# Prompt attention of a hybrid decoder step: which operand of the probability–value product is stationary, and who scales and gates its result

## The chip, the cores and the metric

The kernel runs on one core of a Trainium2 chip. The metric is the device time of one execution in microseconds; the median of three runs is quoted. The core has a matrix engine (TensorE, "PE" in the profile, its weight loads "PEld"), VectorE ("DVE"), ScalarE ("ACT"), GpSimd ("POOL") and a queue engine that issues transfers ("SP"). A matmul takes one operand as stationary weights, loaded by a LDWEIGHTS, and streams the other, the moving one, through them.

## The reference, cut to what matters

For every prompt token an indexer chooses 256 earlier tokens; attention then runs over the chosen ones only. Each query head (8 heads, 2 key/value heads, 128 wide) is normalised by its softmax, and the result is gated by `silu(z_b)`:

```python
logits = einsum('btkgd,btnkd->btkgn', qg, k_sel) * HEAD_DIM ** -0.5
logits = where(valid, logits, NEG_INF)
p = softmax(logits, axis=-1)
o = einsum('btkgn,btnkd->btkgd', p, v_sel)
...
branch_b = attend(q, qi, wi, k, v, ki) * silu(z_b)
merged = sigmoid(g_a) * (branch_a @ w_pa) + sigmoid(g_b) * (branch_b @ w_pb)
```

The sequence has 2048 tokens and the model is 1024 wide. Beside the prompt, 8 sequences of 8 new tokens with a paged cache go through the same layer.

## The kernel before

The prompt is worked through in four tiles of 512 tokens (t = 0 to 3). For each tile TensorE runs 97 products of the big projections, the indexer, and the attention stage that the change touches. Instead of gathering the chosen keys, the kernel computes dense causal logits and adds a mask.

The attention stage of a tile has 16 units u: four query blocks of 128 tokens times four pairs of heads. A unit of query block b of tile t sees n = 4t + b + 1 key blocks of 128, so over the four tiles there are 544 pairs of a unit and a key block. For each unit:

- TensorE forms the logits of both heads (`head_logits`), in pieces of up to 512 keys in three rotating PSUM banks; VectorE adds the mask, writes them to `LP` and takes the row maximum (`mask_logits`, L1835, L1840); ScalarE exponentiates (L900) and sums each row (`SUM`).
- TensorE turns the probabilities, 128x128 at a time, by matmuls with the identity (`turn_p`, L1053, tile `LP`), two key blocks (four turns) to a chunk; ScalarE (L924) or VectorE (L1872) copies each chunk from PSUM to one of three buffers `T`.
- TensorE multiplies (`head_values`): the values `V` of a key block are stationary and the turned probabilities of both heads, 256 columns, are moving (tile `T,V`). The result is already transposed, head dimension by tokens, in columns 0 to 255 of PSUM bank 6 or 7. All of this is plain fp32, for which the trace shows two loads and two matmuls for each call; the big projections are split by hand into high and low halves and show one load and one matmul for each.
- Division by the row sum: VectorE takes the reciprocal `RIN` and builds two diagonal matrices `DG` (L1863); TensorE multiplies them with a matrix of ones (tile `DG,ones`), which spreads 1/sum over all partitions into columns 256 to 511 of the bank; ScalarE copies that to `RB` (L908); VectorE multiplies result and `RB` into `BB` (`finish`, L1846); GpSimd multiplies `BB` by the gate `SZB` (`attn_gate`, L2115).

Each engine has its own program, with semaphores between them; the order on each engine is the order of the text. On TensorE it is `head_logits(u+1)`, inside which the first chunk of unit u is turned, and then `head_values(u)`. On VectorE it is `mask_logits(u+1)`, reciprocal, `DG`, VectorE's share of the copies of unit u, `finish(u-1)`, and, in the first eight units of the last tile, a part of the mask selection of a later block (`choose`, L1754 to L1760).

After the last unit `attn_high` (ScalarE, L942) and `attn_low` (GpSimd L2126, VectorE L1885) split `BB` into `BBH` and `BBL`, eight slices k of which two belong to each head pair, and TensorE goes on with the products `pb` (tile `BBH,WLH`), slice after slice. GpSimd takes slices 0 and 2, then the gate of the last unit, then 4 and 6. The loading of the next tile's input waits for `attn_z`, the mark of the gate of the last unit.

Of the kernel before, what the change touches and what calls it, by code (L numbers as in the profile page):

```python
# [33 lines left out]
ALU = mybir.AluOpType  # L34
# [3 lines left out]
P = 128  # L38
# [72 lines left out]
def program(nc, ins, outs, plan):  # L111
# [78 lines left out]
    DG = [at(f"DG{i}", [P, 256], F32, rJ + 2048 + 1024 * i) for i in range(2)]  # L190
# [111 lines left out]
    for u in range(NSEQ // 2 + 1):  # L302
        for c in range(4):
# [40 lines left out]
    qk, logits, row_max, expd, diag, p_t, p_copy, p_copy_a, pv, rb, rb_copy, attn, attn_z = (  # L344
        signal(n) for n in ("qk", "logits", "row_max", "expd", "diag", "p_t", "p_copy", "p_copy_a", "pv", "rb",
                            "rb_copy", "attn", "attn_z"))
# [270 lines left out]
    def _(act):  # L617
# [275 lines left out]
        def attend(t):  # L893
            for u in range(len(UNITS) + 1):
# [8 lines left out]
                if u >= 1:  # L903
                    v = u - 1
                    act.wait_ge(*rb.at(t, v))
                    if v >= 2:
                        act.wait_ge(*attn.at(t, v - 2))
                    act.activation(RB[v % 2][:, :], ps[6 + v % 2][:, 256:512], ACT.Copy).then_inc(*rb_copy.mark(t, v))  # L908
# [122 lines left out]
    def _(pe):  # L1031
# [364 lines left out]
        def head_values(t, u):  # L1396
# [9 lines left out]
            for c in range(groups):  # L1406
# [3 lines left out]
                if c == 0:  # L1410
                    claim(acc)
                for kk in range(min(2, n - 2 * c)):
                    k = 2 * c + kk
                    ins_ = mm(ps[acc][:, 0:256], V[:, k, (pr // 2) * HD:(pr // 2 + 1) * HD],
                              T[p_slot(t, u, c)][:, kk * 256:(kk + 1) * 256], k == 0, k == n - 1)
                ins_.then_inc(*pv.mark(t, u, c))
            pv.values[t, u] = pv.n
            pe.wait_ge(*diag.at(t, u))
            mm(ps[acc][:, 256:512], ones[:, :], DG[u % 2][:, :]).then_inc(*rb.mark(t, u))
            freed[acc] = attn.at(t, u)  # L1420
# [20 lines left out]
        for t in range(TILES):  # L1441
# [18 lines left out]
            for u in range(len(UNITS)):  # L1460
                if u + 1 < len(UNITS):
                    head_logits(t, u + 1)
                head_values(t, u)
            for f in range(KC):
# [21 lines left out]
    def _(dve):  # L1486
# [355 lines left out]

        def finish(t, u):
            blk, pr = UNITS[u]
            dve.wait_ge(*rb_copy.at(t, u))
            dve.tensor_tensor(BB[:, 2 * pr:2 * pr + 2, blk * P:(blk + 1) * P],  # L1846
                              ps[6 + u % 2][:, 0:256].rearrange("p (h q) -> p h q", h=2),
                              RB[u % 2][:, :].rearrange("p (h q) -> p h q", h=2), ALU.mult).then_inc(*attn.mark(t, u))

        def attend(t):  # L1850
            dve.wait_ge(*gate_mul.at(t, KC - 1, "P"))

            dve.wait_ge(*product.at(len(GEMMS) // TILES * t + len(PROJ_A) + len(PROJ_B) - 1, last_part(t)))
            mask_logits(t, 0)
            for u in range(len(UNITS)):
# [4 lines left out]
                if u >= 2:  # L1860
# [376 lines left out]
```

## Time and profile before

| | |
|---|---|
| median of three runs | 3474.61 us (3470.73 to 3475.79) |
| profiled execution, its own time | 3464.39 us |
| its span, first to last instruction | 3462.5 us |
| mean granted TensorE clock | 0.983 of full speed |
| busy: PE / PEld / DVE / ACT / POOL | 96% / 78% / 61% / 34% / 26% |

Busy times of PE come from modelled ends, which overlap: what one matmul takes from the engine is read from the distance between two starts. In a timeline, a line with "xN" stands for N instructions, and its length reaches from the first start to the last end.

### The profile page before, as it was taken

How to read it: one execution, taken by the hardware profiler on the slowest of the kernel's cores; microseconds unless marked ns; L12 is line 12 of the kernel's file. 1: busy time of each engine (PE TensorE's matmuls, PEld its weight loads, DVE VectorE, ACT ScalarE, POOL GpSimd, SP SyncE). 2: the span in 40 equal slices, each digit the busy share in tenths (PEclk: the TensorE clock that was granted, in tenths of full speed). 3: DMA queues.
4: the chain of work that ended last, by engine and by line, in shares of the span. 5: the costliest groups of instructions: out<-in, count | busy, mean ns of one | idle time of the engine just before them, and what ended most of it. 6: DMA issues, size and time to landing. Idle time of an engine off the chain costs nothing.

```text
span 3462.5 us, 44323 instructions
## 1 busy us (share of the span) xinstructions
PE 3323.2 (96%) x16733; PEld 2704.4 (78%) x16733; DVE 2105.5 (61%) x3980; ACT 1167.2 (34%) x2141; POOL 886.0 (26%) x833
## 2 busy tenths in 40 slices
PE   7899999997889999999999999999999999999999
PEld 6778888864678788888777688888877588878887
DVE  3463399412553799404526999725525999997652
ACT  2345433333532422116412521144322722115531
POOL 2225574443550033101310132011210033110111
PEclk9999999999999999999999999999999999999999
DMA  8556576776377455661465255630375055660007
GB/s 231 181 194 200 171 244 228 258 252 225 110 239 234 138 182 192 211 225 39 168 202 195 87 194 200 231 126 12 111 232 196 33 192 192 215 224 10 10 20 239
DMA packets 281013, 592.29 MB, mean 171 GB/s; under 512 B 17725, under 2 KB 199159, under 8 KB 231138
## 3 DMA queue, kind: packets, MB, share of 16 engines
q1 hardware_dynamic: 270434, 551.70, 47.3%
q0 software_dynamic: 10368, 37.75, 3.2%
q8 instruction: 135, 2.21, 0.3%
q14 instruction: 76, 0.62, 0.1%
HBM read 448.93 MB, written 140.47 MB: 170 GB/s over the span
## 4 chain that ended last, share of the span: by engine, by line
PE 77%; DVE 13%; ACT 3%; DMA 3%; issue 2%; POOL 1%; SPq 1%; ACTq 0%; DVEq 0%; POOLq 0%
PE ps L1048 71%; DVE JUNK L1730 7%; PE ps L1053 6%; DVE SC L1672 1%; DMA WR<-in_w_in 1%; ACT T L717 1%; DVE SMALL L1734 0%; ACT sKPT L846 0%; POOL BBL L2126 0%; DMA GB<-gb_scratch 0%; DVE GE L1732 0%; DVE PFX L1756 0%; DMA WR<-in_w_proj_b 0%; SPq L440 0%; ACT JUNK L636 0%
## 5 line engine op out<-in xcount | busy, mean ns | idle before, releaser
L1048 PE MATMUL ps<-HTH,WLH 128*128 128x512 f32 x4672 | 1478.0, 393 | 0.0
L1048 PEld LDWEIGHTS ps<-HTH,WLH 128*128 128x128 f32 x4672 | 878.6, 188 | 187.2 <-issue 6.5
L1048 PE MATMUL ps<-HTL,WLH 128*128 128x512 f32 x2336 | 910.4, 390 | 0.0
L1730 DVE TENSOR_SCALAR_CACHE_REDUCE JUNK<-SC,SMALL 128x384 bf16<-128x384 f32 (+13 forms) x392 | 579.9, 1479 | 15.7 <-POOL sSC L2047 1.8
L1048 PEld LDWEIGHTS ps<-HTL,WLH 128*128 128x128 f32 x2336 | 439.5, 188 | 94.1 <-issue 6.5
L1835 DVE CUSTOM_DVE_ANT_0 LP<-ps,SC 128x512 f32<-128x512 f32 (+3 forms) x320 | 187.5, 609 | 344.9 <-PE ps L1048 281.8
L787 ACT ACTIVATE T<-ps 128x512 f32<-128x512 f32 x192 | 115.2, 600 | 691.7 <-PE ps L1048 691.7
L1985 POOL TENSOR_TENSOR WLH<-WR,WLH 128x1024 fp32r<-128x1024 f32 x97 | 233.4, 2406 | 404.2 <-ACT WLH L626 403.9
L1048 PE MATMUL ps<-T,V 128*128 128x256 f32 x1088 | 282.8, 387 | 5.6 <-ACT T L924 5.5
L1048 PEld LDWEIGHTS ps<-T,V 128*128 128x128 f32 x1088 | 187.3, 191 | 34.4 <-ACT T L924 12.6
L626 ACT ACTIVATE WLH<-WR 128x1024 fp32r<-128x1024 f32 x97 | 102.7, 1059 | 287.7 <-DMA WR<-in_w_in 209.6
L1605 DVE RECIPROCAL RS<-RS 128x512 f32<-128x512 f32 x40 | 134.1, 3351 | 89.4 <-ACT RS L701 89.2
L924 ACT ACTIVATE T<-ps 128x512 f32<-128x512 f32 (+1 forms) x200 | 115.7, 580 | 198.8 <-PE ps L1053 197.8
L1053 PE MATMUL ps<-ident,LP 128*128 128x128 f32 x1088 | 167.1, 275 | 4.4 <-ACT LP L900 4.4
L1048 PE MATMUL ps<-BBH,WLH 128*128 128x512 f32 x512 | 162.4, 393 | 7.0 <-POOL BBL L2126 6.9
L1048 PE MATMUL ps<-MGH,WLH 128*128 128x512 f32 x512 | 166.7, 398 | 0.0
L717 ACT ACTIVATE T<-ps 128x512 f32<-128x512 f32 (+3 forms) x304 | 153.9, 549 | 33.1 <-DVE QI L1651 8.3
L1048 PE MATMUL ps<-BAH,WLH 128*128 128x512 f32 x512 | 164.0, 392 | 0.0
L1672 DVE SCALAR_TENSOR_TENSOR SC<-T,WI,SC 128x512 f32<-128x512 f32 (+3 forms) x266 | 161.2, 676 | 2.8 <-ACT T L717 1.4
L1053 PEld LDWEIGHTS ps<-ident,LP 128*128 128x128 f32 x1088 | 135.0, 141 | 33.3 <-DVE SMALL L1835 4.7
L2039 POOL TENSOR_SCALAR_AFFINE_SELECT SC<-SC 128x128 f32<-128x128 f32 x16 | 4.6, 292 | 605.7 <-DVE SMALL L1718 605.4
L900 ACT ACTIVATE LP<-LP,SMALL 128x128 f32<-128x128 f32 (+15 forms) x128 | 152.3, 1194 | 4.9 <-DVE SMALL L1840 4.7
(316 smaller groups left out, 5045.8 us busy)
## 6 DMA issues: line engine op xcount, KB each, us to landing
WLH<-w_scratch SPq DMA_DIRECT2D x291, 1024.0 KB, 4.8
w_scratch<-WLH SPq DMA_DIRECT2D x97, 1024.0 KB, 6.3
WR<-in_w_in SPq DMA_DIRECT2D x73, 512.0 KB, 4.4
MW<-in_w_mod SPq DMA_DIRECT2D x24, 512.0 KB, 7.2
XN<-in_x_prompt SPq DMA_DIRECT2D x4, 2048.0 KB, 7.9
q_scratch<-QO SPq DMA_DIRECT2D x32, 256.0 KB, 5.6
ma_scratch<-T SPq DMA_DIRECT2D x32, 256.0 KB, 5.6
gb_scratch<-GB SPq DMA_DIRECT2D x32, 256.0 KB, 6.4
```

The costliest lines, as they stand in the source:

```text
L626: act.activation(WH[j % 3][:, :, :], WR[j % 3][:, :, :], ACT.Copy).then_inc(*w_high.mark(j))
L717: act.activation(T[1 + r % 4][:, 0:n], ps[bank("idx", t, b, h, c)][:, 0:n], ACT.Relu).then_inc(*relu.mark(r))
L787: act.activation(dst, src, func).then_inc(*evac.mark(j, p))
L900: ins_ = act.activation(row, row, ACT.Exp, bias=NM[:, u % 2, hh:hh + 1], accum_out=SUM[:, u % 2, hh:hh + 1])
L924: act.activation(T[p_slot(t, u, c)][:, 0:m], ps[bank("tr", t, u, c)][:, 0:m], ACT.Copy).then_inc(*p_copy_a.mark(t, u, c))
L1048: return pe.matmul(out, lhsT, rhs, start=start, stop=stop, **more)
L1053: return pe.transpose(out, in_, ident[a:a + n, a:a + n])
L1605: link(dve.reciprocal(rs, rs))
L1672: dve.scalar_tensor_tensor(dst, x, w, dst, ALU.mult, ALU.add).then_inc(*scored.mark(r))
L1730: link(dve.tensor_scalar(JUNK[0:n, 0:row.shape[1]], row, MID[0:n, c:c + 1], 0.0, ALU.is_ge, ALU.add, accum_out=CNT[0:n, c:c + 1]))
L1835: ins_ = dve.tensor_tensor_reduce(LP[:, u % 2, hh, c:c + n], ps[bank("qk", t, u, hh, c)][:, 0:n], scores(t)[:, blk, c:c + n], 1.0, -3e38, ...
L1985: pool.tensor_tensor(WL[j % 3][:, :, :], WR[j % 3][:, :, :], WH[j % 3][:, :, :].bitcast(F32), ALU.subtract).then_inc(*w_split.mark(j))
```

## The change

The operands of the probability–value product change places: the turned probabilities of one head (128x128) are stationary, and the values of a key block (128 columns) are moving. The result now stands tokens by head dimension, so that 1/sum is a scalar of each partition. VectorE scales it so while copying it to a buffer `OB` (`scale`), TensorE turns it back (`turn_out`, two turns for each unit), and VectorE gates it with `SZB` while moving it to `BB` (`finish`). The diagonals, the matmuls with ones, ScalarE's copies to `RB` and GpSimd's gate are gone. At the start of the stage VectorE waits for `evac` in place of `product` of the last projection, since `finish` now reads `SZB`.

```diff
-    DG = [at(f"DG{i}", [P, 256], F32, rJ + 2048 + 1024 * i) for i in range(2)]
+    OB = [at(f"OB{i}", [P, 256], F32, rJ + 2048 + 1024 * i) for i in range(2)]
...
-                if u >= 1:
-                    v = u - 1
-                    act.wait_ge(*rb.at(t, v))
-                    if v >= 2:
-                        act.wait_ge(*attn.at(t, v - 2))
-                    act.activation(RB[v % 2][:, :], ps[6 + v % 2][:, 256:512], ACT.Copy).then_inc(*rb_copy.mark(t, v))
...
                 for kk in range(min(2, n - 2 * c)):
                     k = 2 * c + kk
-                    ins_ = mm(ps[acc][:, 0:256], V[:, k, (pr // 2) * HD:(pr // 2 + 1) * HD],
-                              T[p_slot(t, u, c)][:, kk * 256:(kk + 1) * 256], k == 0, k == n - 1)
+                    for hh in range(2):
+                        ins_ = mm(ps[acc][:, hh * HD:(hh + 1) * HD], T[p_slot(t, u, c)][:, (2 * kk + hh) * P:(2 * kk + hh + 1) * P],
+                                  V[:, k, (pr // 2) * HD:(pr // 2 + 1) * HD], k == 0 and hh == 0, k == n - 1, skip_group_check=True)
                 ins_.then_inc(*pv.mark(t, u, c))
             pv.values[t, u] = pv.n
-            pe.wait_ge(*diag.at(t, u))
-            mm(ps[acc][:, 256:512], ones[:, :], DG[u % 2][:, :]).then_inc(*rb.mark(t, u))
-            freed[acc] = attn.at(t, u)
+
+        def turn_out(t, u):
+
+            acc = 6 + u % 2
+            pe.wait_ge(*scaled.at(t, u))
+            for hh in range(2):
+                ins_ = turn(ps[acc][:, 256 + hh * P:256 + (hh + 1) * P], OB[u % 2][:, hh * HD:(hh + 1) * HD])
+            ins_.then_inc(*turned.mark(t, u))
+            freed[acc] = attn_z.at(t, UNITS[u])
...
                     head_logits(t, u + 1)
+                if u:
+                    turn_out(t, u - 1)
                 head_values(t, u)
+            turn_out(t, len(UNITS) - 1)
...
+        def scale(t, u):
+            dve.wait_ge(*pv.at(t, u))
+            for hh in range(2):
+                ins_ = dve.tensor_scalar(OB[u % 2][:, hh * HD:(hh + 1) * HD], ps[6 + u % 2][:, hh * HD:(hh + 1) * HD],
+                                         RIN[:, u % 2, hh:hh + 1], None, ALU.mult)
+            ins_.then_inc(*scaled.mark(t, u))
+
         def finish(t, u):
             blk, pr = UNITS[u]
-            dve.wait_ge(*rb_copy.at(t, u))
+            dve.wait_ge(*turned.at(t, u))
             dve.tensor_tensor(BB[:, 2 * pr:2 * pr + 2, blk * P:(blk + 1) * P],
-                              ps[6 + u % 2][:, 0:256].rearrange("p (h q) -> p h q", h=2),
-                              RB[u % 2][:, :].rearrange("p (h q) -> p h q", h=2), ALU.mult).then_inc(*attn.mark(t, u))
+                              ps[6 + u % 2][:, 256:512].rearrange("p (h q) -> p h q", h=2),
+                              SZB[:, 2 * pr:2 * pr + 2, blk * P:(blk + 1) * P], ALU.mult).then_inc(*attn_z.mark(t, UNITS[u]))
...
-            dve.wait_ge(*product.at(len(GEMMS) // TILES * t + len(PROJ_A) + len(PROJ_B) - 1, last_part(t)))
+            dve.wait_ge(*evac.at(len(GEMMS) // TILES * t + len(PROJ_A) + len(PROJ_B) - 1, last_part(t)))
...
                 link(dve.reciprocal(RIN[:, u % 2, :], SUM[:, u % 2, :]))
-                if u >= 2:
-                    dve.wait_ge(*rb.at(t, u - 2))
-                for hh in range(2):
-                    ins_ = dve.tensor_scalar(DG[u % 2][:, hh * P:(hh + 1) * P], ident[:, :], RIN[:, u % 2, hh:hh + 1], None, ALU.mult)
-                ins_.then_inc(*diag.mark(t, u))
+                if u:
+                    finish(t, u - 1)
...
-                if u:
-                    finish(t, u - 1)
                 for b, r in late_runs(t, u):
                     choose(t, scores(t)[:, b, 0:width(BLOCKS * t + b)], P, b, b, r)
+                scale(t, u)
...
-        def attn_gate(t, u):
-            blk, pr = UNITS[u]
-            pool.wait_ge(*attn.at(t, u))
-            x = BB[:, 2 * pr:2 * pr + 2, blk * P:(blk + 1) * P]
-            pool.tensor_tensor(x, x, SZB[:, 2 * pr:2 * pr + 2, blk * P:(blk + 1) * P], ALU.mult).then_inc(*attn_z.mark(t, UNITS[u]))
...
             attn_low(t, 2)
-            attn_gate(t, len(UNITS) - 1)
             attn_low(t, 4)
```

## Rows read from the trace of the kernel before

**Rows 1.** The profile page: the span, and busy time of PE.

```profile
span 3462.5 us, 44323 instructions
PE 3323.2 (96%) x16733; PEld 2704.4 (78%) x16733; DVE 2105.5 (61%) x3980; ACT 1167.2 (34%) x2141; POOL 886.0 (26%) x833
```

**Rows 2.** Windows, the attention stages of tiles 0 and 3: length, busy times, clock.

```profile
core 0: us, PE busy (x) PEld busy (x) DVE busy (x) ACT busy (x) POOL busy (x), PEclk, DMA share, GB/s
866.00:937.00 71.00, 58.55 (x288) 46.91 (x288) 40.56 (x162) 46.57 (x129) 33.81 (x44) 0.90 0.25 81
...
3110.00:3366.00 256.00, 246.97 (x1345) 210.12 (x1346) 167.38 (x455) 126.31 (x186) 24.56 (x31) 0.98 0.05 15
```

**Rows 3.** Timeline, inside a unit of tile 3: start, length, engine, operation.

```profile
3343.15 0.60 PE L1053 MATMUL ps<-ident,LP 128*128 128x128 f32 x4
...
3343.59 1.03 PE L1048 MATMUL ps<-T,V 128*128 128x256 f32 x4
...
3344.45 0.60 PE L1053 MATMUL ps<-ident,LP 128*128 128x128 f32 x4
```

**Rows 4.** Timeline, the end of a unit of tile 3: matmuls with ones, next turns.

```profile
3352.01 0.59 PE L1048 MATMUL ps<-DG,ones 128*128 128x256 f32 x2
...
3352.45 1.04 PE L1053 MATMUL ps<-ident,LP 128*128 128x128 f32 x8
```

**Rows 5.** Groups by form over the whole span: count, busy us, mean ns.

```profile
L1048 PE MATMUL ps<-T,V 128*128 128x256 f32 x1088 | 282.8, 387 | 5.6 <-ACT T L924 5.5
...
L1048 PE MATMUL ps<-DG,ones 128*128 128x256 f32 x128 | 39.9, 394 | 3.7 <-DVE DG L1863 3.4
...
L2115 POOL TENSOR_TENSOR BB<-BB,SZB 128x256 f32<-128x256 f32 x64 | 49.5, 774 | 336.3 <-DVE BB L1846 336.1
...
L1863 DVE TENSOR_SCALAR DG<-ident,SMALL 128x128 f32<-128x128 f32 x128 | 38.0, 338 | 2.3
...
L908 ACT ACTIVATE RB<-ps 128x256 f32<-128x256 f32 x64 | 24.3, 380 | 66.0 <-PE ps L1048 65.9
```

**Rows 6.** Timeline, three places: loads and matmuls with few moving columns.

```profile
42.41 7.16 PE L1048 MATMUL ps<-MW,SCT 128*9 128x128 f32 x64
...
878.12 0.27 PE L1048 MATMUL ps<-KLOW,QHIGH 128*128 128x128 f32 x1
...
878.23 0.28 PE L1048 MATMUL ps<-KHIGH,QLOW 128*128 128x128 f32 x1
...
880.86 0.28 PE L1048 MATMUL ps<-KLOW,QHIGH 128*128 128x256 f32 x1
...
880.98 0.29 PE L1048 MATMUL ps<-KHIGH,QLOW 128*128 128x256 f32 x1
...
881.99 0.30 PEld L1048 LDWEIGHTS ps<-T,V 128*128 128x128 f32 x2 [0.36 <-ACT T L924]
```

**Rows 7.** Waits of TensorE, attention stage of tile 0: us in total, times, longest.

```profile
PE ps L1048 <- DVE DG L1863: 3.4, 5, 1.1
```

**Rows 8.** Timeline, two places in tile 3: VectorE behind the end of a unit.

```profile
3335.62 0.59 PE L1048 MATMUL ps<-KHIGH,QHIGH 128*128 128x512 f32 x1
...
3336.82 0.69 DVE L1835 CUSTOM_DVE_ANT_0 LP<-ps,SC 128x512 f32<-128x512 f32 x1 [2.13 <-PE ps L1048]
...
3168.25 0.69 DVE L1835 CUSTOM_DVE_ANT_0 LP<-ps,SC 128x512 f32<-128x512 f32 x1 [3.57 <-PE ps L1048]
```

**Rows 9.** One line's instructions: VectorE's scaling in the sample attention, ns min/median/max.

```profile
L1793 DVE TENSOR_SCALAR RB<-ps,SMALL x4: 349/350/351, 798.3 to 862.6; 128x128 f32<-128x128 f32 x4
```

**Rows 10.** Timeline, from the last unit of tile 3 to the product `pb`.

```profile
3363.81 3.52 POOL L2126 TENSOR_TENSOR BBL<-BB,BBH 128x512 fp32r<-128x512 f32 x2
...
3365.73 0.47 PE L1048 MATMUL ps<-BBH,WLH 128*128 128x512 f32 x1 [1.57 <-POOL BBL L2126]
...
3367.29 1.18 POOL L2115 TENSOR_TENSOR BB<-BB,SZB 128x256 f32<-128x256 f32 x1
...
3369.76 0.50 PE L1048 MATMUL ps<-BBH,WLH 128*128 128x512 f32 x1 [0.72 <-POOL BBL L2126]
```

More of the change, by code:

```diff
@@ L343, in program @@
         signal(n) for n in ("u_ready", "taps", "conv", "ba_high", "ba_ready", "gate_mul"))
-    qk, logits, row_max, expd, diag, p_t, p_copy, p_copy_a, pv, rb, rb_copy, attn, attn_z = (
-        signal(n) for n in ("qk", "logits", "row_max", "expd", "diag", "p_t", "p_copy", "p_copy_a", "pv", "rb",
-                            "rb_copy", "attn", "attn_z"))
+    qk, logits, row_max, expd, p_t, p_copy, p_copy_a, pv, scaled, turned, attn_z = (
+        signal(n) for n in ("qk", "logits", "row_max", "expd", "p_t", "p_copy", "p_copy_a", "pv", "scaled", "turned", "attn_z"))
     k_high, k_split, k_whole = (signal(n) for n in ("k_high", "k_split", "k_whole"))
@@ L2186, in _ @@
                     split_low(AFTER_PAGES[u - 4])
-                if u:
-                    attn_gate(t, u - 1)
                 if u == len(UNITS) - 2 and t + 1 < TILES:
```

## The prediction, as it was put on record

> **What bounds the kernel now.** I read the page first: TensorE is busy for 3323.2 of 3462.5 us [rows 1], and the reader is to see that hardly any other engine's time can matter unless TensorE waits for it. Then the windows of the four attention stages: 71, 126, 186 and 256 us, 639 us together, of which the first and the last are shown [rows 2]. TensorE is busy for 247 of 256 us in the last, but only for 58.6 of 71 us in the first, so tile 0 is the one with waits. Since busy times overlap, I then took distances between starts in a timeline. In a full chunk of tile 3, four turns take 3343.59 - 3343.15 = 0.44 us, 0.11 each, and the four probability–value matmuls 3344.45 - 3343.59 = 0.86 us, 0.215 each [rows 3]; together 1.30 us without a gap. So the stage is priced by counting TensorE's instructions, and beyond that only the waits in tile 0 and the hand-over after the last unit are worth reading.
>
> **The probability–value product.** Before: 1088 matmuls of 256 columns [rows 5] at 0.215 us, 233.9 us. After: each becomes two, since a stationary block holds one head: 2176 matmuls of 128 columns, each with its own load, where there were 1088 loads. The columns streamed are the same, but loads double, so the price hangs on whether a load still hides. The trace of before does not show this form (fp32, a full 128x128 load, 128 moving columns). Its parts are there. With a load of only 9 columns, 64 fp32 matmuls of 128 columns take 7.16 us, first start to last end, and one lasts 0.27: (7.16 - 0.27) / 63 = 0.109 us each, the streaming alone. Two full fp32 loads, `T,V`, take 0.30 us, of which one lasts 0.19: the second starts 0.11 us after the first, the loading alone. Split-half matmuls with a full load and 128 columns start 878.23 - 878.12 = 0.11 us apart; with 256 columns 880.98 - 880.86 = 0.12 us [rows 6]. The latter is the pattern in which streaming and loading are equally long, as they would be here, and it shows some friction. Bounds: 0.109 (237.2 us, +3.3) and 0.12 (261.1 us, +27.2). I take 0.111, close to the three rows at 0.11, because the fp32 `T,V` rows at 0.215 for two passes over 256 columns show no friction with the loads beside them: 241.5 us, +7.6.
>
> On whether loads hide at all, the 0.11 us of the split-half matmuls with 128 columns answers: loading 0.11 and streaming 0.06 (half of the 256-column distance) one after the other would be 0.17. A sentence of the Trainium skill speaks against this change: its page "TensorE: Matmul & The Clock Gate", section "The mechanism" of Part 3, says that a weight load overlaps running matmuls only where it targets another row group, and every load here fills all rows. By that rule the sum would be that of the third rival; the trace does not agree, by the 0.11 us.
>
> **The matmuls with ones go.** 64 pairs, 128 matmuls [rows 5], 3352.45 - 3352.01 = 0.44 us each [rows 4]: 28.2 us. In the last unit of each tile TensorE stands waiting for GpSimd right behind the pair [rows 10], so there its removal gives nothing: 28.2 - 1.8 = -26.4 us.
>
> **The turns back come.** 64 pairs at 0.22 us, by the turns of the chunk [rows 3]: 14.1 us; those of the four last units lie in the same wait (0.9): +13.2 us. They need `scaled(u-1)`. Behind them on TensorE stand the turns and values of unit u, for which the copies on ScalarE and VectorE wait. VectorE scales as soon as the values of u-1 end, while TensorE runs all logits of unit u+1, so the wait should cost nothing. Bounds: nothing saved or lost below, and one exposed scaling above (next paragraph).
>
> **VectorE.** Two diagonals of 0.34 us mean [rows 5] go, two scalings from PSUM of 0.35 us [rows 9] come; `finish` keeps its form and moves ahead of the copies. Cover for the scalings: after the end of a unit VectorE sits idle for 2.13 us until the first piece of the next logits is there, 1.2 us after that piece started (3335.62 and 3336.82) [rows 8]; 0.70 us fits, in the units with selection work too (idle 3.57 us). Without that cover 0.7 us of each unit would be late, and behind it in VectorE's queue the masking, which frees the banks of the logits. That masking waits for the same `pv` anyway, so no order is tightened. `finish` waits for `turned(u-1)`, which TensorE gives right after the logits that VectorE has just masked; behind it stand only the copies of the fourth and later chunks, 2.6 us away (two chunks of 1.30). The wait for `evac` instead of `product` ends before the first logits can be masked. All of it: 0.
>
> **ScalarE and GpSimd.** 64 copies of 0.38 us and 64 gates of 0.77 us go [rows 5]. Neither engine sets the pace inside the stage (34% and 26% busy over the span [rows 1]), so I cost them at 0 except at the two places below. The marks move to VectorE; the load of the next tile's input gets its mark earlier, which is counted at 0 too.
>
> **Waits in tile 0.** TensorE waited 3.4 us, five times, for the diagonals [rows 7]: short units, where VectorE finished them after the values were done. The diagonal leaves the loop; the next thing that is late is the exponentials of the following unit. Bounds 0 and about -7 (if the turns of the next unit come forward too); I take -3.4 us.
>
> **Hand-over to the product `pb`.** GpSimd's gate of the last unit (1.18 us) stands between slices 2 and 4, and TensorE waits for slice 4: 0.72 us idle, at 3369.76 [rows 10]. Without the gate slice 4 comes 1.2 us earlier. The first wait, 1.57 us for slice 0, stays. I take -1 us a tile, -4 us; bounds 0 and -7 (new scaling, turn and `finish` in the way, or both waits shortened).
>
> **Sum** against the profiled execution: 7.6 - 26.4 + 13.2 - 3.4 - 4.0 = -13.0 us: span 3462.5 to 3449.5, own time 3464.39 to 3451.4. The profiled execution lies 10.2 us under the median of the runs, 3474.61, so the difference is carried over: 3461.6 us, 0.37% faster. About 0.2%, 7 us, is what a measurement of this kernel can tell from no change.
>
> **Rivals.**
> *Friction.* The new matmuls run at 0.12, not 0.111: 2176 x 0.009 = 19.6 us more, net +6.6, about 3481; at 0.1155, +9.8, net -3.2, 3471. For it: the 256-column row [rows 6]. Against it: `T,V` at 0.215. From 0.114 on, the change is within 0.2%; from 0.117 on, it loses.
> *A new wait in each unit (the other side).* The pair of turns waits for the scaling: the place is `turn_out(u-1)` before the first values of unit u. If VectorE reaches the scaling late by more than the slack, the price is up to 0.7 us in 60 units, +42 us, net +29, about 3504; the point from which it decides is 0.22 us a unit (13.0 / 60), 0.33 us for slower by 0.2%. For it: one engine now does scaling, masking and gating in a row. Against it: 2.13 and 3.57 us idle [rows 8].
> *Loads in the open.* If a full load does not hide behind the preceding matmul, each of 2176 costs 0.11 + 0.109 = 0.219 us: 476.5 us, 242.6 more than before, net 222 more: about 3697. Against it: the 0.11 us above.
> *More waits fall than counted.* Tile 0 gives 7 and the hand-over 7 us, spacing 0.109: net -24, about 3451. For it: 12.4 us of tile 0's 71 in which PE isn't busy [rows 2].
> That the change doesn't do what it says I don't count: the matmuls with ones and the gate are in the trace, and the code drops them.
>
> **Chances.** Forecast 0.62; more waits fall 0.08; friction 0.20 (0.18 of it within 0.2%, 0.02 slower); new wait 0.06; loads in the open 0.04. Faster by over 0.2%: 0.70; within: 0.18; slower: 0.12. The range reaches from the fourth rival, 3450, to friction's middle and some exposed waits, 3477; beyond it lie the loads in the open, most of the new wait and the worst of friction, together less than 2 in 10.
>
> **What would show it.** In the profile after: 2176 matmuls with `V` moving, starts 0.11 us apart; a chunk of 1.30 to 1.34 us; no `DG,ones`; two turns with `OB` behind the logits, without a wait before them; VectorE idle before the first mask of a unit, down from 2.13 to about 1.4 us; the `BBH` matmul of slice 4 without its wait. The prediction is wrong if the starts are 0.115 us apart or more, if TensorE waits for `OB` in most units, or if the hand-over has grown.

## The result, and the profile after

| | median | runs | ratio to before |
|---|---|---|---|
| before | 3470.73 us | 3464.61 to 3475.79 | |
| after | 3451.07 us | 3440.03 to 3453.31 | 0.9937 [0.9916, 0.9958] |

The change makes the kernel 0.63% faster; two repetitions below give 0.48 and 0.55%. The forecast was faster, by 0.37% against its anchor. In microseconds the three pairs of medians differ by 19.7, 16.9 and 18.5, where the sum was 13.0: the direction held, the size was short by 4 to 7 us. The anchor, the median of three runs, was itself high: it was 3474.61, and the medians of all later series of the kernel before lie between 3465.66 and 3470.73. The 3451 that was measured so lies further from the 3461.6 that was forecast than the error in the change is.

In the code of after, lines are shifted: matmul L1041, turn L1046, `scale` L1850, `finish` L1857, mask L1839, ScalarE's copy L917, split on GpSimd L2127. The page of the profiled execution (3440.03 us), span and busy times:

```profile
span 3438.2 us, 46327 instructions
PE 3303.0 (96%) x17821; PEld 2735.4 (80%) x17821; DVE 2115.0 (62%) x3980; ACT 1144.2 (33%) x2077; POOL 838.3 (24%) x769
```

Against [rows 1] the matmuls rose by 1088, as they should (1088 more with `V`, 128 turns for 128 with ones); GpSimd lost its 64 gates and ScalarE its 64 copies. Windows of the attention stages of tiles 0 and 3, columns as in [rows 2]:

```profile
859.50:922.50 63.00, 52.37 (x368) 46.93 (x368) 37.98 (x162) 40.16 (x111) 22.70 (x29) 0.92 0.33 101
3089.50:3341.50 252.00, 244.53 (x1808) 226.83 (x1808) 165.60 (x450) 121.05 (x170) 11.35 (x15) 0.99 0.05 15
```

These windows were set by hand and don't begin and end at the same instructions; what the stages took is in the table below, from starts. Inside a unit of tile 3, start, length, engine, operation:

```profile
3317.16 0.38 PE L1046 MATMUL ps<-ident,OB 128*128 128x128 f32 x2
3317.37 0.60 PE L1046 MATMUL ps<-ident,LP 128*128 128x128 f32 x4
3317.81 1.06 PE L1041 MATMUL ps<-V,T 128*128 128x128 f32 x8
3318.70 0.60 PE L1046 MATMUL ps<-ident,LP 128*128 128x128 f32 x4
```

A chunk now takes 3318.70 - 3317.37 = 1.33 us, where [rows 3] had 1.30; the eight value matmuls 0.89 us, 0.111 each. The two turns of `OB` take 0.21 us and have no wait in front of them. Groups by form over the whole span, then VectorE at the end of the unit before that (start, length, in brackets the idle time):

```profile
L1041 PE MATMUL ps<-V,T 128*128 128x128 f32 x2176 | 286.3, 277 | 5.3 <-ACT T L917 5.2
...
L1850 DVE TENSOR_SCALAR OB<-ps,SMALL 128x128 f32<-128x128 f32 x128 | 39.0, 346 | 97.5 <-PE ps L1041 97.5
...
L1046 PE MATMUL ps<-ident,OB 128*128 128x128 f32 x128 | 25.3, 279 | 5.6 <-DVE OB L1850 5.6
```

```profile
3311.31 0.61 DVE L1850 TENSOR_SCALAR OB<-ps,SMALL 128x128 f32<-128x128 f32 x2 [1.25 <-PE ps L1041]
3312.12 0.69 DVE L1839 CUSTOM_DVE_ANT_0 LP<-ps,SC 128x512 f32<-128x512 f32 x1 [0.20 <-PE ps L1041]
```

The scaling lies in VectorE's idle time, as costed: of the 2.13 us of [rows 8] it uses 0.61, and 1.25 + 0.20 = 1.45 stay idle. TensorE's waits in tile 0's stage (engine, line, waited for: us, times, longest):

```profile
PE ps L1041 <- ACT T L917: 4.5, 6, 1.8
...
PE ps L1046 <- DVE OB L1850: 1.4, 2, 0.7
```

The 3.4 us for `DG` of [rows 7] are gone. What has come is two waits of 0.7 us for `OB`, and so in every tile, 5.6 us in all: those of the last two units, behind whose values no logits stand that would cover the scaling. Last, the hand-over of tile 3:

```profile
3340.38 0.61 DVE L1850 TENSOR_SCALAR OB<-ps,SMALL 128x128 f32<-128x128 f32 x2 [1.25 <-PE ps L1041]
3340.43 6.37 POOL L2127 TENSOR_TENSOR BBL<-BB,BBH 128x512 fp32r<-128x512 f32 x4 [48.66 <-PE ps L1041]
3340.91 1.33 DVE L1892 TENSOR_TENSOR BBL<-BB,BBH 128x512 fp32r<-128x512 f32 x1
...
3341.84 0.47 PE L1041 MATMUL ps<-BBH,WLH 128*128 128x512 f32 x1 [0.35 <-POOL BBL L2127]
```

GpSimd splits its four slices in one go, the gate of 1.18 us in [rows 10] no longer among them, and the first wait of TensorE, 1.57 there, is two of 0.70 and 0.35 us.

The table shows what each stage takes, from starts in the traces of two executions of before and three of after (the repetitions are told below): "attention" from the first logits to the last value matmul, "hand-over" from there to the last matmul of `pb`.

| us | before | before | after | after | after | difference of means | forecast |
|---|---|---|---|---|---|---|---|
| tile 0 attention | 66.95 | 66.97 | 58.12 | 58.94 | 59.21 | -8.2 | -6.1 |
| tile 0 hand-over | 62.44 | 62.60 | 59.72 | 58.63 | 60.34 | -3.0 | -1.0 |
| tile 1 attention | 119.00 | 118.99 | 115.56 | 115.57 | 115.58 | -3.4 | -1.8 |
| tile 2 attention | 182.89 | 182.91 | 181.84 | 181.88 | 181.85 | -1.0 | -1.0 |
| tile 3 attention | 252.91 | 252.09 | 250.16 | 250.76 | 250.84 | -1.9 | -0.05 |
| hand-overs, tiles 1 to 3, each | 47.2 | 47.1 | 46.1 | 46.1 | 46.1 | -1.0 | -1.0 |

The last column splits the terms of the sum by units and key blocks of each tile. Tile 2 and the hand-overs of tiles 1 to 3 came as forecast. The excess sits in tile 0, in tile 1 and at tile 3. Outside these stages the traces differ by several us in either direction (the first logits of tile 0 start between 863.3 and 870.6), so the table adds to more (-20.6) than the medians show.

### The profile page after: what moved, and what is told of

Same layout as the page of the kernel before. It is cut to its first block, busy times and chain, and to the rows that moved or that the text cites. A ratio compares the mean times of both kernels' runs of the same rounds, so it can differ in the third digit from the quotient of the medians.

```text
span 3438.2 us, 46327 instructions
## 1 busy us (share of the span) xinstructions
PE 3303.0 (96%) x17821; PEld 2735.4 (80%) x17821; DVE 2115.0 (62%) x3980; ACT 1144.2 (33%) x2077; POOL 838.3 (24%) x769
## 4 chain that ended last, share of the span: by engine, by line
PE 77%; DVE 13%; ACT 3%; DMA 2%; issue 2%; POOL 1%; SPq 1%; ACTq 0%; DVEq 0%; POOLq 0%
PE ps L1041 71%; DVE JUNK L1734 7%; PE ps L1046 6%; DVE SC L1676 1%; ACT T L716 1%; DMA GB<-gb_scratch 0%; DVE SMALL L1738 0%; POOL BBL L2127 0%; ACT sKPT L845 0%; DVE GE L1736 0%; ACT JUNK L635 0%; DVE XN L1545 0%; DMA sXN<-in_x_sample 0%; SPq L439 0%; DVE PFX L1760 0%
## 5 line engine op out<-in xcount | busy, mean ns | idle before, releaser
L1041 PE MATMUL ps<-HTH,WLH 128*128 128x512 f32 x4672 | 1479.1, 393 | 0.0
L1041 PEld LDWEIGHTS ps<-HTH,WLH 128*128 128x128 f32 x4672 | 878.7, 188 | 187.3 <-issue 6.5
L1041 PE MATMUL ps<-HTL,WLH 128*128 128x512 f32 x2336 | 910.7, 390 | 0.0
L1041 PEld LDWEIGHTS ps<-HTL,WLH 128*128 128x128 f32 x2336 | 439.8, 188 | 93.8 <-issue 6.5
L1839 DVE CUSTOM_DVE_ANT_0 LP<-ps,SC 128x512 f32<-128x512 f32 (+3 forms) x320 | 187.5, 608 | 225.2 <-PE ps L1041 161.3
L1041 PE MATMUL ps<-V,T 128*128 128x128 f32 x2176 | 286.3, 277 | 5.3 <-ACT T L917 5.2
L1041 PEld LDWEIGHTS ps<-V,T 128*128 128x128 f32 x2176 | 263.7, 192 | 9.8 <-ACT T L917 8.4
L917 ACT ACTIVATE T<-ps 128x512 f32<-128x512 f32 (+1 forms) x200 | 115.5, 580 | 265.3 <-PE ps L1046 265.0
L1046 PE MATMUL ps<-ident,LP 128*128 128x128 f32 x1088 | 166.4, 274 | 4.7 <-ACT LP L899 4.5
L1041 PE MATMUL ps<-MGH,WLH 128*128 128x512 f32 x512 | 166.4, 397 | 0.0
L1041 PE MATMUL ps<-BBH,WLH 128*128 128x512 f32 x512 | 162.4, 392 | 1.3 <-POOL BBL L2127 1.1
L2115 POOL TENSOR_TENSOR QLOW<-QU,QHIGH 128x256 fp32r<-128x256 f32 x64 | 48.1, 754 | 471.9 <-ACT QHIGH L890 471.9
L1041 PE MATMUL ps<-BAH,WLH 128*128 128x512 f32 x512 | 163.1, 389 | 0.0
```

Of the source, the lines that this page charges most:

```text
L917: act.activation(T[p_slot(t, u, c)][:, 0:m], ps[bank("tr", t, u, c)][:, 0:m], ACT.Copy).then_inc(*p_copy_a.mark(t, u, c))
L1041: return pe.matmul(out, lhsT, rhs, start=start, stop=stop, **more)
L1046: return pe.transpose(out, in_, ident[a:a + n, a:a + n])
L1839: ins_ = dve.tensor_tensor_reduce(LP[:, u % 2, hh, c:c + n], ps[bank("qk", t, u, hh, c)][:, 0:n], scores(t)[:, blk, c:c + n], 1.0, -3e38, ...
```

## The experiments

**Both kernels again.** Unchanged, on another chip.

> The kernel before, unchanged, run again for the granted clock of each execution. The sum of instructions gave -13 us for the change, measured were about -20 us in the median. Theory 1 (clock): the executions of before have a lower mean granted clock than those of after (0.984 in the median); before is expected at 0.980 to 0.982 in its median, and span x (1 - clock) carries the rest: executions of equal clock lie 11 to 14 us apart. Theory 2 (waits): the clocks of both kernels have the same median within 0.001, and at equal clock they still lie about 20 us apart, because waits in tile 0 and at the hand-over were priced too low. Theory 3 (scatter): the median of these new executions moves by 5 us or more from 3470.7, so that the true difference may be 13 us after all.

> The changed kernel, unchanged, run again. Theory 1: median clock 0.984, ratio to before 0.994 to 0.995, and a second profile that has more half-clock stretches than the first (clock 0.983 to 0.984, span about 3450) with its extra time just there. Theory 2: the same ratio, but the profile's attention stages are as short as in the first profile (58, 116, 182, 250 us) also where the clock falls. Theory 3: ratio 0.996 or above.

Measured: before 3467.88 us, 1.0005 [0.9995, 1.0015] of the pooled 3468.23; after 3451.30, 0.9952 [0.9938, 0.9966]. A third series of after gave 3450.67, 0.9945 [0.9932, 0.9959]:

> The kernel after, unchanged, a third time, to narrow the size of the change: the two earlier ratios are 0.9937 [0.9916, 0.9958] and 0.9952 [0.9938, 0.9966]. If the forecast's sum (-13.0 us, 0.9963) was short by only a few us, this gives 0.994 to 0.996 (-21 to -14 us); if the sum was right and the earlier runs were lucky, 0.996 to 0.997.

The three lie at -21.9, -16.6 and -19.1 us by their ratios; the sum's -13.0 lies inside the second interval only. So the sum was short.

The granted clock of each execution tells how much of that is clock. The executions with a clock on record, 90 of before and 15 of after on several chips, lie 17.3 us apart in the mean. Those of equal clock lie 14.8 us apart (at 0.983: 19 of before, 2 of after), 14.7 (at 0.984: 20 and 8) and 11.9 (at 0.985: 13 and 3). Within each kernel an execution was 2.3 us shorter for each 0.001 of clock, and after has 0.0015 more in the mean: 3.4 of the 17.3 us. So the end of Theory 1 came true, 11 to 14 us at equal clock, about 14 in all, though its level for before did not: the median is 0.983. The 20 us at equal clock of Theory 2 and the shift of 5 us of Theory 3 fall. The forecast has no term for the clock, and without the clock's part its -13.0 is nearly the whole.

**The gate back on GpSimd** (in the kernel after; VectorE's `finish` becomes a copy).

```diff
-            dve.tensor_tensor(BB[:, 2 * pr:2 * pr + 2, blk * P:(blk + 1) * P],
-                              ps[6 + u % 2][:, 256:512].rearrange("p (h q) -> p h q", h=2),
-                              SZB[:, 2 * pr:2 * pr + 2, blk * P:(blk + 1) * P], ALU.mult).then_inc(*attn_z.mark(t, UNITS[u]))
+            dve.tensor_copy(BB[:, 2 * pr:2 * pr + 2, blk * P:(blk + 1) * P],
+                            ps[6 + u % 2][:, 256:512].rearrange("p (h q) -> p h q", h=2)).then_inc(*attn.mark(t, u))
...
+            attn_gate(t, len(UNITS) - 1)
```

> The changed kernel with the gate put back on GpSimd (VectorE copies the turned result to BB, GpSimd multiplies by SZB, slices 4 and 6 behind the gate of the last unit). By the prediction's hand-over term it loses 1 us a tile, +4 us against the changed kernel, 8 to 9 us faster than before. Theory 2 (hand-over priced too low): +7 us or more. Theory 1: +4 us from waits, and in tile 0 perhaps a half-clock stretch behind the longer wait, which costs 1.7 us more.

3455.64 us, 0.9964 [0.9950, 0.9977]: 4.3 us slower than after by the medians, though the intervals of the two overlap. At the hand-over of tile 3 the old wait is back:

```profile
3358.07 1.18 POOL L2121 TENSOR_TENSOR BB<-BB,SZB 128x256 f32<-128x256 f32 x1
...
3360.98 0.50 PE L1041 MATMUL ps<-BBH,WLH 128*128 128x512 f32 x1 [1.15 <-POOL BBL L2132]
```

`pb` takes 45.5 us in tiles 1 to 3, where after has 44.4, and the hand-over of tile 0 takes 60.99, where after has 59.6 in the mean. That is 4.8 us together. So in the kernel after the place of the gate is worth 4 to 5 us, and it shows at the hand-over, as costed.

**No division** (in the kernel before: no diagonals, no matmuls with ones, no copies to `RB`; the division by the row sum is left out).

```diff
-            pe.wait_ge(*diag.at(t, u))
-            mm(ps[acc][:, 256:512], ones[:, :], DG[u % 2][:, :]).then_inc(*rb.mark(t, u))
```

> The kernel before without the division by the row sum: no diagonals, no matmuls with ones, no copies to RB, the result goes to BB undivided; values stay stationary and the gate stays on GpSimd. By the prediction's terms 26.4 + 3.4 = 29.8 us faster than before (ratio 0.9914). Theory 2 (waits in tile 0 priced too low): 35 us or more faster. Theory 1: 30 us plus what the clock gives, with a tile 0 that shows fewer half-clock stretches; per stage the profile gives -6.6 us in each of tiles 1 to 3 at equal clock.

3436.07 us, 0.9910 [0.9896, 0.9924]: -32 us, where the terms of the removed work were worth -29.8. The attention stages of tiles 2 and 3 are 176.50 and 244.31 us, 6.4 and 8.2 shorter than before (mean of the two); 6.6 is what 15 pairs of 0.44 us make. The 8.2 hold a shorter wait at tile 3's start, which is told below.

**No turn back** (in the kernel after; the output of each head stays unturned and is gated as it is).

```diff
-            for hh in range(2):
-                ins_ = turn(ps[acc][:, 256 + hh * P:256 + (hh + 1) * P], OB[u % 2][:, hh * HD:(hh + 1) * HD])
...
-                              ps[6 + u % 2][:, 256:512].rearrange("p (h q) -> p h q", h=2),
+                              OB[u % 2][:, :].rearrange("p (h q) -> p h q", h=2),
```

> The changed kernel without the two turns of each unit: VectorE gates the scaled result straight from OB into BB, so the output is not turned back. By the prediction's term 13.2 us faster than the changed kernel, about 3438 us, 3.3 us in each attention stage. Theory 1: the same, since the turns showed 0.109 us each and no wait of weight from tile 1 on (tile 0: up to 5 us of wait for the chunk copy lies behind them and stays). Theory 2 (the turns hide under the wait for the first chunk's copy): clearly less, 5 to 9 us, least in tile 0 and in the blocks whose last piece of logits is short.

3443.29 us, 0.9930 [0.9916, 0.9943]: 8 us faster than after by the medians, less than the 13.2 that the term costs. Tile 2's attention is 178.65 us, 3.2 below after, which is the size of the term (3.3 a tile); but `pb` grew from 44.4 to 45.3 us in tiles 1 to 3, and the hand-over of tile 0 from 59.6 to 62.44. The reason for the first stands in the hand-over of tile 3:

```profile
3344.89 1.52 DVE L1853 TENSOR_TENSOR BB<-OB,SZB 128x256 f32<-128x256 f32 x1
...
3348.16 0.50 PE L1041 MATMUL ps<-BBH,WLH 128*128 128x512 f32 x1 [1.01 <-DVE BBL L1888]
```

With both inputs in SBUF and GpSimd at work beside it, `finish` takes 1.52 us; with one in PSUM, in after, 0.41. Inside the units it takes 0.42 in either kernel. The turn into PSUM pays a part of its price back there.

**The gate on VectorE alone** (in the kernel before: GpSimd's product becomes a second one of VectorE, and VectorE waits for `evac` at the start of the stage, as in the change).

```diff
+            dve.wait_ge(*attn.at(t, u))
+            dve.tensor_tensor(x, x, SZB[:, 2 * pr:2 * pr + 2, blk * P:(blk + 1) * P], ALU.mult).then_inc(*attn_z.mark(t, UNITS[u]))
...
-            attn_gate(t, len(UNITS) - 1)
```

> The kernel before with one part of the change alone: VectorE multiplies by the gate SZB right behind its product with RB, GpSimd's gate is gone; diagonals and stationary values stay. By the prediction's hand-over term -1 us a tile, -4 us, ratio 0.9988. Theory 1: -4 to -5 us, gap and pb of tiles 1 to 3 from 47.1 to about 46.1 us each. Rival: the second VectorE product takes the place of the gate on the path (0.4 us more on VectorE in each unit and at the end), so that less than 2 us is left.

3466.04 us, 0.9996 [0.9986, 1.0006]: not to be told from no change. `pb` of tiles 1 to 3 fell from 44.76 to 44.10 us, which is the wait for slice 4 ([rows 10], 0.72); the first wait stayed, 1.57 us. The hand-over of tile 0 fell from 62.5 to 61.02. So in the kernel before the gate's move alone gives 0.66 us in each of three hand-overs, not 1.0, and 1.5 in tile 0; the whole is too small for the interval. The change as a whole gives 0.39 in `pb` of tiles 1 to 3 and 0.61 in the first wait, from 2.38 to 1.77 us between the last value matmul and the first of `pb`.

**Clock: tile 0's waits filled in the kernel before.** The granted clock dips to 0.50, the lower of its levels (1.2 GHz), for some us behind waits of TensorE. The rival for the excess: fewer waits, fewer dips. Throw-away matmuls stand in the waits for the diagonals of units 0 to 7 and behind the last unit.

```diff
+            if t == 0 and u < 8:
+                for _ in range(2):
+                    mm(ps[acc][:, 256:256 + P], ones[:, :], ident[:, :], skip_group_check=True)
             pe.wait_ge(*diag.at(t, u))
...
+            if t == 0:
+                fill(6, 9)
```

> The kernel before with throw-away matmuls in TensorE's waits of tile 0: four before each wait for the diagonals in units 0 to 7 and eighteen after the last unit. Nothing else is changed, and no result uses them. Both profiles of before show a half-clock stretch of 3.4 us 26 us into tile 0's attention stage and one at its hand-over, both profiles of after show neither. Theory 1 (clock): the two stretches vanish, tile 0's attention stage goes from 67.0 to about 65.3 us and hand-over with pb from 62.5 to about 60.8, 3 to 4 us together, although TensorE does more work. Theory 2 (only the waits count): no gain, the stage stays at 67 us or grows by the up to 0.4 us a unit where the wait is shorter than the fill.

3466.42 us, 0.9997 [0.9989, 1.0006]: nothing gained. The dip went; windows of 5 us, 25.5 us behind the first logits of tile 0 (columns as in [rows 2]; granted clock is third from the end), of the kernel before (its repetition) and of the filled one:

```profile
889.63:894.63 5.00, 3.84 (x15) 3.35 (x15) 2.47 (x10) 1.77 (x5) 2.21 (x3) 0.66 0.00 0
```

```profile
891.41:896.41 5.00, 3.42 (x20) 2.88 (x20) 3.93 (x10) 2.85 (x9) 3.68 (x4) 1.00 0.09 26
```

But the stage took 67.91 us against 66.97, and the hand-over 65.77 against 62.60. In the stage TensorE's waits for the chunk copies (`T`) rose from 4.9 to 5.4 us, and the throw-away matmuls take TensorE's time where the waits did. Theory 1 fell: here the end of a dip inside a stage that waits for other engines was no gain.

**Clock: three long waits filled, in both kernels.** The waits before the first logits of tile 0, before the fourth piece of the first logits of tile 3, and in the turning of the next tile's input.

```diff
+            if t == 0:
+                fill(3, 15)
             head_logits(t, 0)
...
+                    if (t, u, hh, c) == (TILES - 1, 0, 0, 3 * TILE):
+                        fill(3 + ring["tr"] % 3, 23)
...
+                if t and k >= 5:
+                    fill(PBANK[j, "P"], {5: 21, 6: 4, 7: 3}[k])
```

> The changed kernel with throw-away matmuls in three long waits that both kernels have: before the first logits of tile 0 (30), before the fourth piece of logits of tile 3 (46), and while the next tile's input is scaled, before the turns of slices 5, 6 and 7 (42, 8, 6, three times). No result uses them. Theory 1 (clock): the half-clock stretches there (10 to 14 us in tile 0, 7 in tile 3, 10, 7 and 7 us behind the turns, in the profiles of after) vanish or shorten; half of some 40 us would be 20 us at most, 8 to 15 us are expected, so 3436 to 3443 us. Theory 2 (the clock doesn't matter here): no change from 3451 or slower by what the fill overruns.

> The kernel before with the same throw-away matmuls in the same three long waits as the filled kernel after (ahead of tile 0's first logits, ahead of the fourth piece of tile 3's first logits, in the turning of the next tile's input); nothing of the change. Theory 1 (the gain of the change is work and waits, the clock adds little to it): the fills are worth about as much here as they were in the kernel after (-7.5 us, granted clock up from 0.984 to 0.990), so about 3467.8 - 7.5 = 3460.3 us, 0.9978, and the filled kernel after stays 13 to 17 us ahead of this one. Rival (the part of the gain beyond the sum is clock that the kernel after gets by having fewer waits): the fills are worth more here, 11 us and up, 3457 us or less, and the filled kernels lie less than 13 us apart.

> The filled kernel after, unchanged, on the chip that also runs the filled kernel before: 3443.8 us by its first run (0.9931 of before). Theory 1: 13 to 17 us under the filled kernel before. Rival: less than 13 us under it.

The filled kernel after: 3443.75 us, 0.9931 [0.9915, 0.9946], and on the second chip 3445.40, 0.9935 [0.9922, 0.9949]. The filled kernel before, on that chip: 3462.15, 0.9979 [0.9969, 0.9989]. So the fills are worth 7.5 and 5.3 us in the kernel after, a little less than the 8 to 15 expected, and 7.0 in the kernel before, and the two filled kernels lie 16.75 us apart by the medians, where the unfilled lie 18.5 on that chip. The rival's 13 us is not excluded by intervals of 3.5 and 4.7 us to either side. That the excess is all clock isn't borne out, but a part is: 1.8 us by these medians, 3.4 by the executions of equal clock. The filled kernel after is the fastest that leaves nothing out. Windows of the first 16 us of tile 3's stage, before and before filled:

```profile
3110.44:3126.44 16.00, 9.22 (x30) 7.30 (x31) 13.00 (x32) 6.95 (x6) 0.00 (x0) 0.68 0.21 71
```

```profile
3109.44:3125.44 16.00, 15.68 (x96) 13.56 (x97) 15.42 (x43) 8.19 (x8) 0.74 (x1) 1.00 0.21 75
```

Of the 66 matmuls more in this stretch 46 are the fill; 20 are useful ones that no longer come behind it, at a clock of 1.00 instead of 0.68. With the fills tile 3's attention takes 249.10 us before and 248.80 after: -0.3, near the -0.05 of the forecast. So the work of the units doesn't hold the 1.9 of the table: it is a wait of TensorE for VectorE's selection at tile 3's start (6.78 us before, 5.39 and 5.57 in after) and the clock behind it. In the filled kernel before, the stretch from tile 3's first logits to the fourth piece also fell, from 9.1 to 7.7 us, without the change; the kernel before without the division waits 5.40 us there, the kernel after without the turn back 7.01. What sets the length wasn't settled, nor whether the change has a hand in it.

**Tile 0's hand-over.** In the trace of before, behind the last matmuls with ones of tile 0, stands a wait that the prediction had not read, because its window ended at 937 (start, length, in brackets idle time):

```profile
933.11 3.22 ACT L942 ACTIVATE BBH<-BB 128x512 fp32r<-128x512 f32 x6
...
934.10 0.59 PE L1048 MATMUL ps<-DG,ones 128*128 128x256 f32 x2
...
936.23 0.38 ACT L908 ACTIVATE RB<-ps 128x256 f32<-128x256 f32 x1
936.64 0.42 DVE L1846 TENSOR_TENSOR BB<-ps,RB 128x256 f32<-128x256 f32 x1 [1.07 <-ACT RB L908]
...
937.16 1.62 PE L1048 MATMUL ps<-WLH,sBB 128*128 128x256 f32 x8 [2.47 <-DVE BB L1846]
```

ScalarE's copy to `RB` stands behind six conversions, VectorE's `finish` behind the copy, and TensorE needs the PSUM bank that `finish` frees. In after no copy by ScalarE lies in this chain. To test it, the copy was moved ahead of four of the conversions, in tile 0 of the kernel before:

```diff
-                    attn_high(t, range(KC - 2))
+                    attn_high(t, range(2 if t == 0 else KC - 2))
+                if t == 0 and u == len(UNITS):
+                    attn_high(t, range(2, KC - 2))
```

> The kernel before, with one order changed in tile 0 alone: ScalarE copies the last unit's reciprocals to RB after two of its six conversions to BBH, not after all six. In the kernel before these conversions take 3.22 us, the matmuls with ones are done while they run, the copy starts behind them (936.23), and TensorE waits 2.47 us for the finish of the last unit before it may go on (937.16). Theory 1 (a part of tile 0's excess is this wait, which the change takes away because no copy by ScalarE lies in the chain any more): the 2.47 us fall to under 1.0; from the last value matmul to the end of product pb the time of tile 0 goes from 62.4 to between 59 and 61 us, as in the kernel after (58.6 to 60.3). In the whole, 1.5 to 3 us, too little to measure: 0.9990 to 1.0000. Rival (the wait only changes its name: the next thing late is the split on GpSimd or VectorE): tile 0's stretch stays above 61.5 us.

3467.78 us, 1.0004 [0.9995, 1.0013]; the hand-over of tile 0 took 61.98 us. The rival held: the wait changed its name.

```profile
937.99 1.43 PE L1050 MATMUL ps<-WLH,sBB 128*128 128x256 f32 x8 [2.16 <-POOL sBB L2121]
```

GpSimd was next. In before its gates wait for VectorE's `finish`, and behind them in its order stand the re-joining of the keys (`KT`, 3.35 us) and the split of the samples' `sBB`. So the re-joining was moved ahead of the gate of unit 13 as well:

```diff
+                if t == 0 and u == len(UNITS) - 2:
+                    whole_keys(t)
                 if u:
                     attn_gate(t, u - 1)
```

> The kernel before with ScalarE's copy early as in the run before, and in tile 0 GpSimd re-joins the keys (KT, eight operations, 3.35 us) ahead of its gate of the third last unit, not behind it; there GpSimd sat idle for 3.80 us waiting for VectorE's finish. Theory 1 (tile 0's hand-over is held by two chains, ScalarE's copy and GpSimd's gates with what stands behind them, and the change takes away both): GpSimd's split of the samples ends 1.5 us and more ahead of where it did (against the last value matmul), TensorE's wait there falls from 2.16 to about 1 us, and tile 0 from the last value matmul to the end of pb goes from 62.0 to 61 us or less. In the whole 1 to 2 us, not to be told from none: 0.9990 to 1.0005. Rival (a third chain of the same length, or the clock alone, sets this stretch): it stays above 61.5 us.

3466.75 us, 0.9999 [0.9989, 1.0008]; the hand-over of tile 0 took 60.62 us, within 0.3 us of the longest of after (60.34).

```profile
935.51 1.19 PE L1050 MATMUL ps<-WLH,sBB 128*128 128x256 f32 x8 [0.98 <-DVE BB L1848]
```

So two chains, one over ScalarE's copy and one over GpSimd's gates, hold the start of `pb` in tile 0: it comes 4.69 us after the last value matmul in before and 2.82 with both chains shortened. The eight matmuls behind the wait span 1.19 us where they took 1.62; there the lower clock has gone too. In the whole, 1.9 us is less than the interval can tell, and the profiled execution lost more at tile 0's start (69.84 us of attention, behind 20.5 us at a clock of 0.50 where before has 10.2).

But this isn't how the change got its -3.0. In after `pb` of tile 0 starts 3.77 us behind the last value matmul, which is 0.95 less than in before. Another 1.0 are waits inside `pb` for `sRAW`, a part of the samples' product that ScalarE copies: 2.4 and 2.6 us in before, 2.1, 1.3 and 1.2 in after. Before, then the second execution of after (the last line of each has KB and us from issue to landing of the weights' load):

```profile
940.79 0.38 SPq L447 DMA_DIRECT2D XN<-in_x_prompt  x1
945.82 0.38 SPq L423 DMA_DIRECT2D WR<-in_w_proj_b  x1
951.82 1.06 ACT L626 ACTIVATE WLH<-WR 128x1024 fp32r<-128x1024 f32 x1 [5.68 <-DMA WR<-in_w_proj_b]
953.20 0.66 PE L1048 MATMUL ps<-PAIR,sRAW 128*128 128x64 f32 x4 [0.94 <-ACT sRAW L663]
...
WR<-in_w_proj_b SPq DMA_DIRECT2D x1, 512.0 KB, 6.0
```

```profile
932.17 0.38 SPq L446 DMA_DIRECT2D XN<-in_x_prompt  x1
939.33 0.38 SPq L422 DMA_DIRECT2D WR<-in_w_proj_b  x1
943.44 1.06 ACT L625 ACTIVATE WLH<-WR 128x1024 fp32r<-128x1024 f32 x1 [3.79 <-DMA WR<-in_w_proj_b]
945.61 0.56 PE L1041 MATMUL ps<-PAIR,sRAW 128*128 128x64 f32 x4
...
WR<-in_w_proj_b SPq DMA_DIRECT2D x1, 512.0 KB, 4.1
```

ScalarE's copy stands behind the conversion of weights (`WR`) that have just been loaded. The load of the next tile's input (`XN`) is issued when the gate of the last unit is done, 6.9 us behind the last value matmul in before and 2.7 in after. In before it is still under way when the weights' load is issued, which then takes 6.0 us to land, against 4.1 in the second execution of after. In all eight executions with the gate on GpSimd this load takes 5.9 to 6.7 us, in six of the seven with the gate on VectorE 3.9 to 4.8, in the seventh (the first of after) 5.9. That the input's load slows the other wasn't tested by itself. The last 1.0 us of the -3.0 goes with the clock in part: both executions of before have a stretch of 3.4 us at 0.50 at the start of this hand-over, of the three of after only the slowest has one.

## Why the prediction was right in direction and wrong in size

- **Which step failed.** The two terms for tile 0 and what was counted at nothing. "I take -3.4 us" for the waits was mis-sized: they cost 5.2. "I take -1 us a tile" failed for the hand-over of tile 0: it gave -3.0, of which 1.0 goes with the load of the next tile's input, whose earlier start was "counted at 0 too". And the sum has no term for the clock, with which 3.4 of the 17.3 us go. Two smaller misses point the other way: the product (+8.7 for +7.6) and a wait for `OB` of 0.7 us a tile.
- **Product.** Right: +7.6 forecast. The median distance is 0.112 us in every tile, against the 0.111 taken and below the 0.114 from which friction would have decided; before it was 0.216, against 0.215. By these medians the term is +8.7. By sums of distances between starts, the value matmuls grew by 2.1 and 3.0 us in tiles 2 and 3, where the term has 2.4 and 3.2. Friction and loads in the open fall: a full load hides behind 128 columns. The Trainium skill's page "TensorE: Matmul & The Clock Gate", section "The mechanism" of Part 3, lets a load overlap running matmuls only where it targets another row group, though the same section also has loads pulled ahead that target a background weight buffer. The 0.112 us doesn't agree with the first; no run here shows the second by itself.
- **Matmuls with ones and turns back.** Right within 1 us a tile: removing the division gave 32 us for 29.8, and 3.2 us a tile came back with the turns, for 3.3.
- **VectorE at 0.** Right but for one unit a tile: the scaling lies in idle time, and only the last two units of a tile wait for `OB`. That of the last lies where a wait was counted; that of the one before it, 0.7 us a tile, had no term. The rival of a new wait in each unit falls: 8 waits, not 60.
- **Hand-over, tiles 1 to 3.** Right: -1.0 each. Its make-up was not: -0.39 is in `pb`, -0.61 ahead of it, in the first wait, which the forecast had left as it was.
- **Hand-over, tile 0.** The four hand-overs were taken for alike and read from tile 3, and the wait behind the last pair was put down to GpSimd in all. Tile 0's is for VectorE (2.47 us), has the samples' product in front of it and waits for the samples and for weights inside `pb`. Of its -3.0, 0.95 lies ahead of `pb`, 1.0 in the waits for `sRAW`, and the last 1.0 is clock in part. The two runs on its order show that its start can be shortened, not that the change did it so.
- **Waits in tile 0.** Mis-sized: -3.4 was the idle time of the view [rows 7], which is counted from a matmul's modelled end. By distances between starts, the 16 steps from the last value matmul of a unit to the first with ones take 8.7 and 8.6 us in the two executions of before, nine of them longer than the 0.216 of a step without a wait; 16 x 0.216 is 3.5, so the diagonals cost 5.2. One of them:

```profile
892.02 0.38 PE L1048 MATMUL ps<-T,V 128*128 128x256 f32 x1
893.49 0.79 PE L1048 MATMUL ps<-DG,ones 128*128 128x256 f32 x1 [1.09 <-DVE DG L1863]
```

Its step is 1.47 us, 1.25 more than 0.216, where the view has 1.09. With 5.2 in place of 3.4, and 0.7 for the new wait for `OB`, the forecast for the stage is -7.2 of the measured -8.2. The last 1.0 stays open; a part of it may be clock (12.7 us at 0.50 in both executions of before, 9.2, 12.4 and 11.9 in after). TensorE's waits for the chunk copies did not come down much: 4.8 us in before, 4.5 in after.

- **No term.** Tile 1's -3.4 instead of -1.8: its first us hold a stretch at 0.50 in before (1570.5 to 1571.5 lies in it) that is not there in the three executions of after, but is in both of the filled kernel after (117.00 us), and isn't in four variants of the kernel before (117.42 to 117.49 us). It costs about 1.6 us and isn't tied to the change; without it on either side the difference is -1.9. Tile 3's -1.9 is told above.

The fourth rival, "more waits fall than counted", had the direction of two of its three parts (5.2 of its 7 us for tile 0's waits, 6 of its 7 for the hand-overs); the spacing of 0.109 was not met. That its 3451 is the number measured is luck: it is -24 from an anchor that was high, and the change is -17 to -20. It got 0.08, because the only wait read behind tile 0's last unit was that of tile 3.

## What to carry to other kernels

Which operand is stationary cost little here, where a load of 128 columns hides behind 128 moving ones (0.112 us, against 0.108 for half of a matmul of 256): choose the side on which scalars lie along partitions, and count what the turning back costs against the helpers that it replaces. Price a wait that is to go by the distance between starts, not by the idle time of a view. When a stage recurs, read its hand-over in each recurrence, and past the end of the window, since the first one may have other work in front of it. Compare executions of equal clock as well as medians. Where an operation leaves an engine that looks idle, look for what stands behind it in that engine's order, and who waits for that, transfers too.

## What the runs showed of the hardware that wasn't expected

- Throw-away matmuls in three long waits raise the mean granted clock from 0.983–0.984 to 0.988–0.990 and save 5 to 7.5 us in either kernel, although TensorE does more work. In and behind such a wait, of 6.78 us at tile 3's start, the clock stands at 0.50 for 7 to 10 us in before, and matmuls of 512 columns start 0.43 us apart there, where they started 0.23 apart ahead of it. Filling the many short waits of tile 0's stage saved nothing.
- Where GpSimd and VectorE each split a slice at a hand-over, the one that started first was the fast one in these kernels. VectorE's slice takes 0.69 us and GpSimd's 1.77 where VectorE starts 0.05 us ahead (before), 1.33 and 1.26 where it starts 0.48 us after GpSimd (after); the first product follows GpSimd's start by 1.92 us [rows 10] and by 1.41 us.
- The same VectorE product costs 0.41 us with one input in PSUM and 1.52 with both in SBUF, GpSimd at work beside it in both cases. Inside the units it takes 0.42 either way.
